# Four layers on one core: fp32 projections against split fp32r projections from a ring of 1 MB units

## What is computed

```python
def first_block(x, ...):                      # layers 0 and 1
    for layer in range(2):
        h = rmsnorm(x, norm_mix_pre[layer])
        m = attention_mixer(h, ...) if layer == 0 else recurrent_mixer(h, ...)   # A, R
        x = x + rmsnorm(m, norm_mix_post[layer])
        f = swiglu(rmsnorm(x, norm_ffn_pre[layer]), ...)                         # F0, F1
        x = x + rmsnorm(f, norm_ffn_post[layer])
# second block, layers 2 and 3
h = h + dilated_diff_mixer(rms_norm(h, attn_norm), ...)                          # E
h = h + swiglu_2(rms_norm(h, ffn_norm), ...)                                     # F2
h = h + hgrn2_mixer(rms_norm(h, hgrn_norm), ...)                                 # G
h = h + moe_swiglu(rms_norm(h, moe_norm), ...)                                   # M: 8 experts, 3584 wide, top 2
```

## Time and profile before

| | |
|---|---|
| three runs | 2328.8, 2330.67, 2332.07 us; median 2330.67 |
| profiled execution | 2333.04 us, its span 2331.3 us |
| PE busy | 2191.8 us, 94% |
| DVE, ACT busy | 1424.3 us (61%), 1194.4 us (51%) |
| mean granted clock of PE | 0.959 of 2.4 GHz |
| M, the experts | 1001.5 us of the span |

### The profile page before, as it was taken

The page is one execution under the profiler, slowest core; times in us unless marked ns, Lnnn a source line. Parts: engine busy times, 40 slices in busy tenths (PEclk is TensorE's granted clock), DMA queues, the critical chain, the costliest instruction groups (busy, mean ns, idle before and its releaser), DMA issues.

```text
span 2331.3 us, 28572 instructions
## 1 busy us (share of the span) xinstructions
PE 2191.8 (94%) x11126; PEld 1797.8 (77%) x11126; DVE 1424.3 (61%) x1256; ACT 1194.4 (51%) x1148; POOL 36.3 (2%) x87
## 2 busy tenths in 40 slices
PE   7988998979998978999897899999999999999998
PEld 5647997759997646998764588888888888888887
DVE  1335543345434364543424488889888888888888
ACT  1344431534332153432734267777677777776775
POOL 2000000000000000000000000000000000000000
PEclk9998998989998979999997799999999999999999
DMA  8305546434554303565420299999999999999997
GB/s 309 109 0 172 180 162 211 141 118 150 175 208 144 109 0 109 176 203 216 145 73 19 104 361 347 363 351 356 355 354 372 339 371 342 368 343 363 350 360 267
DMA packets 216998, 535.76 MB, mean 230 GB/s; under 512 B 9469, under 2 KB 79262, under 8 KB 216942
## 3 DMA queue, kind: packets, MB, share of 16 engines
q1 hardware_dynamic: 213936, 530.61, 63.4%
q0 software_dynamic: 1088, 4.19, 0.5%
q10 hardware_dynamic: 1918, 0.18, 0.1%
HBM read 533.90 MB, written 1.05 MB: 229 GB/s over the span
## 4 chain that ended last, share of the span: by engine, by line
PE 84%; ACT 8%; DVE 5%; issue 2%; POOL 0%; DMA 0%; ACTq 0%; DVEq 0%; POOLq 0%
PE ps L1700 12%; PE ps L1702 12%; PE ps L1701 11%; PE ps L431 8%; PE ps L548 6%; PE ps L549 6%; PE ps L550 6%; PE ps L458 5%; PE ps L435 3%; ACT ring_r L1691 3%; PE ps L563 3%; PE ps L564 3%; PE ps L565 3%; PE ps L1710 1%; PE ps L1753 1%
## 5 line engine op out<-in xcount | busy, mean ns | idle before, releaser
L1696 DVE TENSOR_TENSOR ring_r<-ring,ring_r 128x2048 fp32r<-128x2048 f32 x339 | 761.7, 2287 | 92.7 <-ACT ring_r L1691 92.7
L1691 ACT ACTIVATE ring_r<-ring 128x2048 fp32r<-128x2048 f32 x339 | 629.1, 1910 | 36.3 <-DMA ring<-in_moe_w_gate 29.3
L1700 PE MATMUL ps<-ring_r,arena_r 128*128 128x512 f32 x1344 | 531.8, 396 | 1.0 <-DVE arena_r L1932 1.0
L1702 PE MATMUL ps<-ring_r,arena_r 128*128 128x512 f32 x1344 | 524.4, 390 | 0.0
L1701 PE MATMUL ps<-ring_r,arena_r 128*128 128x512 f32 x1344 | 524.2, 390 | 0.0
L1702 PEld LDWEIGHTS ps<-ring_r,arena_r 128*128 128x128 f32 x1344 | 252.7, 188 | 54.6
L1700 PEld LDWEIGHTS ps<-ring_r,arena_r 128*128 128x128 f32 x1344 | 252.8, 188 | 51.5 <-issue 1.1
L1701 PEld LDWEIGHTS ps<-ring_r,arena_r 128*128 128x128 f32 x1344 | 253.1, 188 | 50.4
L431 PE MATMUL ps<-arena,ring 128*128 128x256 f32 x1152 | 259.6, 387 | 7.4 <-DVE arena L374 5.3
L431 PEld LDWEIGHTS ps<-arena,ring 128*128 128x128 f32 x1152 | 223.2, 194 | 43.3 <-DVE arena L374 6.6
L549 PE MATMUL ps<-arena_r,ring_r 128*128 128x256 f32 x816 | 233.4, 286 | 0.0
(11 more groups left out here) (326 smaller groups left out, 2758.7 us busy)
## 6 DMA issues: line engine op xcount, KB each, us to landing
ring<-in_moe_w_gate SPq DMA_DIRECT2D x115, 1024.0 KB, 5.1
ring<-in_moe_w_up SPq DMA_DIRECT2D x112, 1024.0 KB, 5.1
ring<-in_moe_w_down SPq DMA_DIRECT2D x112, 1024.0 KB, 4.9
ring<-in_ffn_w_gate SPq DMA_DIRECT2D x33, 1024.0 KB, 7.3
ring<-in_ffn_w_up SPq DMA_DIRECT2D x33, 1024.0 KB, 9.7
ring<-in_ffn_w_down SPq DMA_DIRECT2D x33, 1024.0 KB, 5.0
ring<-in_attn_w_in SPq DMA_DIRECT2D x12, 2048.0 KB, 12.5
ring<-in_hgrn_w_in SPq DMA_DIRECT2D x8, 2048.0 KB, 9.8
```

What stands on the lines that cost most here:

```text
L1691: nc.scalar.activation(unit_parts(k)[0], ring[:, slot_of(k), 0:2048], ACT.Copy).then_inc(m_hi, 1)
L1696: nc.vector.tensor_tensor(low, ring[:, slot_of(k), 0:2048], high, ALU.subtract).then_inc(m_lo, 1)
L1700: nc.tensor.matmul(out_, x[:, 0, f, :], w[0], start=first, stop=False)
L1702: return nc.tensor.matmul(out_, x[:, 0, f, :], w[1], start=False, stop=last)
```

## The change

All weights up to the experts are now fp32r in three products. The ring has five units of 1 MB. A unit is copied (high, L299, ACT) and subtracted in place (low, L308, DVE) in stream order, up to three units ahead of the product; its load waits for the unit five before it. Each norm works per token tile, with the gain as a row that is repeated over the partitions. `first_tokens` begins each stage with tile 0's products of its first two to four units; the transposes of the next norm's tile 0 stand before the last quarter of the output product. The activations of the output products are split too (`out_high`, `out_low`). A, E and G project v first; E's last two units are of kind F. The feed-forward parts are written out without the loop (7539 rows of PE instead of 2741). M's code is as before, but its first loads wait for the last units of the ring before it.

```diff
@@ the stream @@
-        def load(pairs, used):
-            s = next_slot()
-            stream.append((s, pairs(s), freed[s]))
+        def unit(shape, src, halves=True):
+            split_no.append(sum(n is not None for n in split_no) if halves else None)
+            weights.append((shape, src))
+            return len(weights) - 1
...
+        slot_raw = lambda u: ring[:, u % NS_EARLY, 0:2048]
+        slot_lo = lambda u: ring_r[u % NS_EARLY][0][:, :]
+        slot_hi = lambda u: ring_r[u % NS_EARLY][1][:, :]
...
+        A_plan = project(A_w_in, several("H", 1024, 2) + several("F", 0, 4) + several("F", 1536, 4) + several("H", 2560, 2))
+        R_plan = project(R_w_in, several("F", 1024, 4) + several("F", 0, 1))
+        R_gate_w = [unit(lambda v: v.rearrange("p (k n) -> p k n", k=KT), a[n][0].rearrange("n (k p) j -> p (n k) j", p=P), False)
+                    for n in ("rg_w_a", "rg_w_i")]
+        R_plan += project(R_w_in, several("F", 256, 3))
+        R_out = project_out(a["rg_w_out"][0])
+        E_plan = project(E_w_in, several("H", 1536, 3) + several("H", 2816, 1) + several("F", 0, 6) + several("F", 2304, 2))
+        G_plan = project(G_w_in, several("H", 2048, 4) + several("F", 1024, 4) + several("F", 0, 4) + several("F", 3072, 4))
@@ splitting and products @@
+        def highs_to(act, last):
+            while high_done[0] <= min(last, N1 - 1):
+                u = high_done[0]
+                high_done[0] += 1
+                if split_no[u] is not None:
+                    act.wait_ge(landed[u % NS_EARLY], landed_at(u))
+                    nc.scalar.activation(slot_hi(u), slot_raw(u), ACT.Copy).then_inc(w_hi, 1)
...
+        def by_columns(pe, u, bank, fs=(0, 1), ts=slice(0, 2)):
...
+            for f in fs:
...
+                for kt in range(KT):
+                    nc.tensor.matmul(o, wh[:, kt, c], HTh[:, ts, kt, :], start=(kt == 0), stop=False)
+                    nc.tensor.matmul(o, wh[:, kt, c], HTl[:, ts, kt, :], start=False, stop=False)
+                    mm = nc.tensor.matmul(o, wl[:, kt, c], HTh[:, ts, kt, :], start=False, stop=(kt == KT - 1))
...
+        def first_tokens(pe, k, pairs):
+            pe.wait_ge(s_htl, 4 * k + 2)
+            for n, (u, bank) in enumerate(pairs):
+                if n == len(pairs) - 1:
+                    norm_turn(pe, k, 1)
+                weights_ready(pe, u)
+                by_tokens(pe, u, bank, (0,))
+            pe.wait_ge(s_htl, 4 * k + 4)
+            for u, bank in pairs:
+                by_tokens(pe, u, bank, (1,)).then_inc(w_used, 1)
...
         def out_tensor(pe, plan, m, high, low):
+            for t in range(TT):
+                for n, (u, r) in enumerate(plan):
+                    if t == 1 and n == 3:
+                        norm_turn(pe, 2 * m + 1, 0)
...
@@ R_scalar, between the sigmoids and the tanh @@
+            highs_to(act, R_out[1][0])
             act.wait_ge(r_sig, KT)
@@ R_vector, between the scan and R_y @@
+            lows_to(dve, R_out[3][0] + 1)
@@ G_scalar and G_vector, at the head of each step of the chain @@
+                highs_to(act, G_plan[4 + u][1] + 3)
...
+                lows_to(dve, G_plan[4 + u][1] + 3)
@@ SP, M's first loads @@
+            for k in range(NU):
+                if k < NS_EARLY:
+                    sp.wait_ge(*used(N1 - NS_EARLY + k))
```

More of the change, by code:

```diff
@@ L236, in project @@
+        landed_at = lambda u: 16 * (u // NS_EARLY + 1)
+        evacs = [0]
         def project(w, parts):
             plan = []
[L238 to L249, removed]
@@ new lines, in ffn_scalar, with gated, high @@
+        def ffn_scalar(act, n, plan, ahead):
+            g, u, d, order = plan
+            h0 = PAIRS_FF * n
+            def gated(i):
+                act.wait_ge(*used(g[i]))
+                if i >= 2:
+                    act.wait_ge(s_v, h0 + i - 1)
+                nc.scalar.activation(silu[:, i % 2, :], ps[:, 2 * (i % 2), :], ACT.Silu).then_inc(s_sg, 1)
+            def high(i):
+                if i < 2:
+                    act.wait_ge(s_ft, 2 * n + i + 1)
+                else:
+                    act.wait_ge(s_v, h0 + i + 1)
+                    act.wait_ge(*used(d[i - 2]))
+                nc.scalar.activation(hidden[:, 0, i % 2, :], ps[:, 2 * i + 1, :] if i < 2 else whole[:, i % 2, :],
+                                     ACT.Copy).then_inc(s_hh, 1)
+            for what, i in order:
+                unit_ = {"g": g, "u": u, "d": d}[what][i]
+                highs_to(act, unit_ + ahead)
+                if what == "g":
+                    gated(i)
+                elif what == "u" and i != 0:
+                    high(0 if i == 1 else i)
+                if (what, i) == ("g", 2):
+                    high(1)
@@ L1191, in E_tensor @@
             pe.wait_ge(const_ok, 2)
[L1192 removed]
+            for j in range(4, 12):
                 unit_tensor(pe, E_plan, j, 2)
@@ L1312, in E_scalar @@
             squares(8)
-            root(8)
-            act.wait_ge(e_qn, 9)
-            first_split_scalar(act, FFN[2])
+            qk_root(8)
+            for q in range(4):
+                out_high(act, 2, q, (OT, (e_ot, 16) if q < 3 else (e_qn, 9)), E_oh)
         def E_vector(dve, step):
-            norm_vector(dve, step, 4)
+            norm_vector(dve, step, 4, E_plan[2][1], E_plan[3][1])
             def normalise(i):
@@ L1478, in G_scalar @@
                 ins.then_inc(g_k, 1)
-            for u in range(4):
-                unit_scalar(act, G_plan, 4 + u, 4, G_q[:, 2 * u:2 * u + 2, :], ACT.Silu)
             def exps(h):
```

1021 lines of the change are left out of this document (479 added, 542 removed).

## The result

The changed kernel takes **2368.9 us** (median of 4 runs, 2367.84 to 2370.7), the one before 2331.27 beside it (4 runs). The ratio is 1.0164, 95% interval 1.0148 to 1.0180: slower by 1.6%, 37.6 us. The forecast was 2357.5, and slower. In the traces the span went from 2331.3 to 2366.5, +35.2.

What follows compares the result with a forecast made beforehand. PE bounds F0, E's projections, output products and M; ACT and DVE set the time in PE's gaps in A, R and G. Stage terms summed to +26.7 us, giving 2357.5 us, range 2315 to 2388.

Steps and rivals of the forecast that it cites:

- A: First attention stage: 12 units save 14.1 us, ACT's small loads, a landing and a split cost more; +2.2 us.
- M's start: G's output product, norm 7 and router: expert units' landing and splits idle PE 10.8 us; +6.1 us.
- R behind the gates: R after its gates: output units' landing delays the tanh, low parts stand between scan and `R_y`; +15.3 us.
- The saving per unit: All projections: a unit takes 5.73 us on PE instead of 6.91, saving 1.18 us each over 48 units.
- R up to the gates' end: R's first part: five units save 5.9 us, but a low part and a landing make PE wait; +3.9 us.
- Norms 2, 4 and 6: Norms behind the feed-forward parts: 2 and 4 gain nothing, 6 costs +2.0 us for units split between its steps.
- Place one: R between gates and `R_y`: 7.8 us for a landing ahead of the tanh, 6.9 for three low parts.
- PE setting G's time: Rival: G's forget chain lies beside the products, so G gains 18.9 us; 2318 us, chance 0.13.
- Landings hidden: Rival: waits for landings in R, A and E are hidden, -18 us; 2340, inside the forecast's own range.
- Small effect: Rival: the sum's plus terms are only half as large, +0 to +5 us in total; chance 0.06.
- Straight code: Rival: without loops, feed-forward instructions come at 0.132 us instead of 0.12, 57 us more; 2414 us, chance 0.07.
- All gains landing on PE: Rival: the whole 81 us saved on PE shows, all four gaps absorbing the splits; 2250 us, chance 0.04.

Runs made afterwards that it cites:

- the run with the gates unblocked: Changed kernel with, in R, unit 4's low part ahead of the convolution and the eighth unit's high part between the sigmoids: 2355.49 us, ratio 1.0113.
- with the bias later: Changed kernel, but POOL issues the 1.5 MB bias and the 0.5 MB gain row behind norm 0: 2367.45 us, ratio 1.0173.
- the first edit in R: Changed kernel with the first two output units' high parts behind the second gate evacuation and their low parts behind the scan: 2366.74 us, ratio 1.0164.
- the control: The changed kernel run once more, unedited, on another chip beside the kernel before: 2369.92 us, ratio 1.0181.

## Why the prediction was right, and where its sizes were off

**The mechanism held.** The sum said that PE's gain (81 us forecast on PE alone) would be lost in A, R and G and at M's start, where ACT and DVE set the time. The runs show each loss at the instruction that was named: the two high parts ahead of the tanh, the low part ahead of a chain step, the v units ahead of the chain, the expert units ahead of the norm. R behind the gates (+15.5 for 15.3), E (-4.9 for -5.9), G (+22.8 for +20.4) and M's start (+5.0 for +6.1) were each within 2.5 us. The total was short by 10.9 us, 29% of the measured change. It is nearer than its terms by luck: in the traces the stretches miss by 18.9 us upward (A 7.4, R up to the gates 7.9, G 2.4, and two small ones) and by 10.2 downward (the norms above all).

**The saving per unit was taken at full clock everywhere.** PE's busy time fell by 57 us and not by 81. Where PE waits between the units, the products behind a wait run at a lower granted clock and save less than 1.18 us each. In A twelve units were to save 14.1 us and PE's busy time fell by 7.4, at a mean clock of 0.89 where it was 0.94 (8 transposes, 1.0 us, are in it). That the clock is the reason is shown only for R, by the run with the gates unblocked.

**R up to the gates' end** was the term that failed most: +3.9 forecast, +11.8 measured. The forecast had 9.8 us of waits in it (4.5 for unit 4's low part, the rest for the landing ahead of the sigmoids and the pace of ACT), and 11.55 were measured. The larger part is the saving: 5.9 us were taken for the five units ahead, but PE was busy for 51.15 us in this stretch where it was 50.80. The run with the gates unblocked gave back 13.2 us of R.

**A** was +9.6 for +2.2. The step priced ACT's small loads at 9.7 of PE idle, of which the run showed about 3.0. It left out that norm 0's first unit lands only at 16.7 us (the first product at 21.1 instead of 16.45, 4.7; with the bias later 2.7 to 3.8 of that came back) and that two low parts stand on the chain of the attention (4.0, by the run with these moved). The 5.3 for a landing ahead of `weights(2)` were 2.9 in the trace.

**Norms 2, 4 and 6** were better than forecast: 0, 0 and +2.0 were taken, but from the last product of the feed-forward part to the next stage's first it is 9.0, 8.8 and 5.7 us, where it was 12.0, 11.9 and 7.3 before. That is 9.7 us better than forecast, and the three stretches of the table together are 9.1 better. Beginning with tile 0 paid even with splits between the two tiles.

**Place one was right in its sum and wrong in its parts.** 7.8 for the landing and 6.9 for the low parts came out as +15.5 together. But removing the first alone gave 4.1, since the splits then came back behind the scan. With the low parts behind the products as well, R took 12.8 us less.

**Rivals.** PE setting G's time: three steps shorter by 2.2 us each shortened G by 6.8, and a chain that began 11.3 us earlier shortened it by 9.0, so the chain set it. Landings hidden: not so, ACT waited for them in R (3.27 ahead of the sigmoids, 3.23 and 0.63 ahead of the tanh) and at M's start. Small effect: refuted. Straight code: 0.12 us a product, refuted. All gains landing on PE: refuted as such, but not for good; with the waits removed the same products end 17.8 us below the kernel before. The Trainium skill, "TensorE: Matmul & The Clock Gate", section "Back-to-back issue gap", has 109 ns for a product of 256 columns that stands alone, and the changed kernel's rows again give 120 in a stream. The other rule that was weighed, the Trainium skill, "DMA: Bandwidth & Descriptors", section "Anatomy of one DMA", is given there for transfers that GpSimd issues; the weights here are issued by SP, so the estimate of 4.4 us for 1 MB that is worked out from it wasn't tested by them. For 1 MB the changed kernel has, in us to landing:

```profile
ring<-in_attn_w_in SPq DMA_DIRECT2D x24, 1024.0 KB, 5.6
ring<-in_hgrn_w_in SPq DMA_DIRECT2D x16, 1024.0 KB, 5.7
```

against 12.5 and 9.8 us for 2 MB before (medians, with other loads in flight). Per MB that is 5.6 against 6.3 in A and E, and 5.7 against 4.9 in G: no later in the one, later in the other. The forecast took 5.1 for all of them.

## What to carry to other kernels

A product that is made cheaper on one engine by work on two others pays only where that engine sets the time; price each stage by what ends its waits, and look at the instruction ahead of which the new work is queued, not at the engine's busy share. The same split was free in one place, 2.2 us in each step of a chain in another, and 13 us with its neighbour where it held back a slot, its load, and the queue that waited for that load: 10 us of waits, and 3 us because the products behind them ran at a lower granted clock. Put such work into the gaps in which its engine waits inside the chain, and when a wait is removed look at once at what that queue must do next: here half the gain of the first edit in R came back as five low parts behind the scan.

## What the runs showed of the hardware

After an idle stretch of PE an fp32r unit takes longer, at a lower granted clock. Two units in G's chain, the first behind 1.0 us of idle time, the second behind 9.7 (the columns of the earlier trace rows):

```profile
1158.60:1164.60 6.00, 5.97 (x48) 5.77 (x48) 3.25 (x8) 3.83 (x4) 0.00 (x0) 1.00 0.61 177
1174.30:1182.90 8.60, 8.56 (x48) 8.36 (x48) 3.85 (x8) 5.78 (x7) 0.00 (x0) 0.66 0.00 0
```

48 products take 6.0 us at clock 1.00, and 8.6 at a mean of 0.66, between the levels of 1.2 and 2.4 GHz. It cost nothing in these steps, as the chain and not PE set the pace; in R up to the gates' end it cost 2.9 us. It is one reason why PE's busy time fell by 57 us and not by 81 (another are the transposes that were added, 7 us by the forecast): a cheaper product saves less when PE has to wait for its operands.

At the start SP issues three loads of 1 MB by 2.8 us, behind the input, and POOL two gain rows and the 1.5 MB bias beside them. The first unit lands after 14.98 us (13.9 in the control), the next two 3.2 and 3.0 us behind it; in M the median is 5.1. With the bias and the second gain row issued later the first unit lands after 9.34. So its place at the head of SP's queue doesn't protect it from transfers of another queue. What the loads behind it in its own queue cost wasn't tried.
